# Convolution taps with their chunks, gates and first adds moved, earlier chunk splits, last tile by row tiles

## The chip, the cores and the metric

One core of one Trainium2 chip runs the whole program. The metric is the time of one execution on the device in microseconds (us). TensorE does matmuls and transposes, VectorE (DVE in the rows), ScalarE (ACT), GpSimd (POOL) and SyncE (SP) work beside it, each in its own order, and semaphores hold one engine until another has got somewhere.

## The reference

A trunk of two layers over 256 rows of width 2048, all in float32. Cut to what matters here:

```python
u = x @ ev_w_in                      # layer 0: 12 column tiles of 512
h = a * sigmoid(gate); h = causal_depthwise_conv(h, width=31)
a_out = silu(layer_norm(h))
b_out = hgrn2(q, f, i, g) * gnorm_g * silu(g)
x = layer_norm(ALPHA * x + concat(a_out, b_out) @ ev_w_out)
x = layer_norm(ALPHA * x + square(relu(x @ w1)) @ w2)
# layer 1: the same, with two kinds of attention heads in place of conv and hgrn2
```

## The kernel before

**Matmuls.** A float32 product is made of three faster ones. Each operand is split into a high part and a rest, and TensorE adds hi x hi, hi x lo and lo x hi (lines 1326 to 1328). Weights stream through in *chunks* of 256 x 512 (512 KB). A chunk s is loaded by SP into one of four raw buffers, ScalarE copies it to `w_hi` (line 493, in the MLP line 716), VectorE subtracts to get `w_lo` (line 802, in the MLP line 1199), and TensorE then does 12 matmuls of 128 x 512 with it, six for each of the two row tiles r (rows 0 to 127 and 128 to 255). SP may load chunk s once `w_lo` of chunk s - 4 is made. Both `w_hi` and `w_lo` of a chunk wait until TensorE is done with the chunk that lay in the same place: chunk s - 4 at first, chunk s - 8 where the ring is eight deep. In layer 0 that begins at chunk 120. `upto(s)` is the call on ScalarE and VectorE that splits every chunk up to s; all their other work is placed by hand between such calls.

**Stages of a layer.** Chunks 0 to 95 are the 12 input tiles. Chunks 96 to 127 are the output projection in three parts: part 0 (chunks 96 to 103, two a tile), part 1 (104 to 119, four a tile) and part 2 (120 to 127). Part 2 uses the last four heads' output, which TensorE transposes behind chunk 117 ("O1", line 1398), ScalarE copies to `c_hi` (line 508, called as `group_hi`) and VectorE completes as `c_lo` (line 814, `group_lo`). Then the MLP: 4 blocks of 8 tiles of 8 chunks, from chunk 128 on. Accumulators are two, used in turn, so that tile t + 2 waits until VectorE has added tile t to X (`add_row`, lines 827 and 830, for both row tiles).

**Beside it in layer 0.** The convolution is 248 *taps* on VectorE (line 1067, 128 x 256 each). `taps_behind(s)` gives how many follow chunk s, four or five, two while the recurrence runs. `forget(half, s0)` turns the forget gates to a cumulative sum: a maximum (line 976), a logarithm on ScalarE (line 575), and a scan on VectorE (line 980). It is called inside the loop at s = 31 and s = 79 and splits two chunks more on its way. The recurrence has seven levels and two more: VectorE makes decays (line 993), weighs (lines 1007 and 1008), TensorE multiplies (line 1481) and VectorE takes the scores (line 1022). `gates(half)` (line 1034) multiplies the output gate by its norm weights, needed at chunk 117.

**MLP.** The first product of a tile is taken out by ScalarE with relu (line 710) and squared (line 712), and TensorE transposes it (line 1712) in the middle of the next tile. A tile's 8 chunks are worked in two halves of four: row tile 0 of the half, then row tile 1 of it.

**End.** `last_norm` (line 926) adds the last tile, takes the statistics, and for each piece of a row tile subtracts the mean (`centre`, line 864) and scales (`scale`, line 870). SP then stores that piece (line 363). `STORES` has two pieces of 1024 columns for row tile 0 and four of 512 for row tile 1. The reciprocal root comes from GpSimd (line 413).

## Time and profile before

| what | us |
|---|---|
| median of 3 runs | 2288.47 |
| their range | 2286.49 to 2291.45 |
| profiled execution | 2288.11 |
| its span, first to last instruction | 2286.4 |
| TensorE busy with matmuls in the span | 2249.9 |
| VectorE busy | 1341.9 |
| ScalarE busy | 1057.0 |
| load of a weight chunk, issue to landing, medians of its groups | 3.7 to 4.7 |

The span leaves out 1.7 us of the execution's time. Matmuls overlap in the rows (each is shown with 0.39 us, and starts about 0.23 us after the one before), so the gap between two starts tells more than the busy time.

### The profile page before, as it was taken

To read this page: it belongs to the slowest core of one execution; us is meant where nothing else is said; L and a number is where in the kernel's file an instruction comes from. 1 tells how busy PE (TensorE), PEld (TensorE's weight loads), DVE (VectorE), ACT (ScalarE), POOL (GpSimd) and SP (SyncE) were. 2 spreads that over 40 slices of the span, in tenths; PEclk is the share of its full clock that TensorE was granted. 3 is DMA by queue.
4 is the path that set the end of the run, shared out by engine and by line. 5 is a ranking of instruction groups with operands and counts; after the bars stand their busy time and mean duration, and the time that the engine had idled before them with its cause. 6 is when DMAs were issued, how large, how long until landed. Compare 5 with 4: busy or idle time off the path is not lost.

```text
span 2286.4 us, 28509 instructions
## 1 busy us (share of the span) xinstructions
PE 2249.9 (98%) x10331; PEld 1864.2 (82%) x10331; DVE 1341.9 (59%) x1472; ACT 1057.0 (46%) x1146; POOL 36.6 (2%) x68
## 2 busy tenths in 40 slices
PE   8999999999999999999999999999999999999997
PEld 7888788788888888888878888887888888888886
DVE  4898986854445544445565445568454454544455
ACT  4555565454344444344434444444534444543541
POOL 2000000000000001000000000000000000000000
PEclk9999999999999999999999999999999999999999
DMA  7555545565556656655546555565555565555553
GB/s 242 166 158 158 172 133 177 164 209 190 196 184 221 194 190 199 207 185 184 186 127 193 166 177 165 164 227 156 190 190 195 184 221 195 183 193 200 184 184 110
DMA packets 213040, 418.50 MB, mean 183 GB/s; under 512 B 12793, under 2 KB 13361, under 8 KB 211904
## 3 DMA queue, kind: packets, MB, share of 16 engines
q1 hardware_dynamic: 211120, 406.90, 55.8%
q0 software_dynamic: 1808, 10.04, 1.3%
q8 instruction: 78, 1.28, 0.2%
q14 instruction: 34, 0.28, 0.0%
HBM read 414.79 MB, written 2.10 MB: 182 GB/s over the span
## 4 chain that ended last, share of the span: by engine, by line
PE 91%; DVE 4%; DMA 2%; ACT 1%; issue 1%; DVEq 0%; SPq 0%; ACTq 0%
PE gemm L1326 29%; PE gemm L1328 29%; PE gemm L1327 29%; PE pair L1712 1%; DVE w_lo L802 1%; DVE lnp L1067 1%; DMA raw<-in_mlp_w 1%; PE pair L1481 1%; ACT w_hi L493 1%; PE pair L1398 1%; PE pair L1438 0%; PE pair L1554 0%; PE pair L1626 0%; PE pair L1599 0%; DVE X L864 0%
## 5 line engine op out<-in xcount | busy, mean ns | idle before, releaser
L1199 DVE TENSOR_TENSOR w_lo<-raw,w_hi 128x1024 fp32r<-128x1024 f32 x488 | 596.7, 1225 | 484.7 <-ACT w_hi L716 453.6
L716 ACT ACTIVATE w_hi<-raw 128x1024 fp32r<-128x1024 f32 x492 | 522.1, 1061 | 631.4 <-PE gemm L1328 608.7
L1326 PE MATMUL gemm<-w_hi,x_hi 128*128 128x512 f32 x1792 | 710.4, 396 | 7.0 <-DVE w_lo L802 6.5
L1328 PE MATMUL gemm<-w_hi,x_lo 128*128 128x512 f32 x1792 | 701.1, 391 | 0.0
L1327 PE MATMUL gemm<-w_lo,x_hi 128*128 128x512 f32 x1792 | 700.3, 391 | 0.0
L1326 PE MATMUL gemm<-w_hi,c_hi 128*128 128x512 f32 x1280 | 502.0, 392 | 4.6 <-DVE X L830 3.4
L1328 PE MATMUL gemm<-w_hi,c_lo 128*128 128x512 f32 x1280 | 499.6, 390 | 0.0
L1327 PE MATMUL gemm<-w_lo,c_hi 128*128 128x512 f32 x1280 | 499.5, 390 | 0.0
L802 DVE TENSOR_TENSOR w_lo<-raw,w_hi 128x1024 fp32r<-128x1024 f32 x280 | 340.3, 1223 | 199.3 <-ACT w_hi L493 193.5
L493 ACT ACTIVATE w_hi<-raw 128x1024 fp32r<-128x1024 f32 x276 | 289.3, 1056 | 305.8 <-PE gemm L1328 268.9
L1326 PEld LDWEIGHTS gemm<-w_hi,x_hi 128*128 128x128 f32 x1792 | 338.0, 189 | 82.3 <-issue 6.1
L1328 PEld LDWEIGHTS gemm<-w_hi,x_lo 128*128 128x128 f32 x1792 | 337.8, 189 | 71.2
L1327 PEld LDWEIGHTS gemm<-w_lo,x_hi 128*128 128x128 f32 x1792 | 338.3, 189 | 66.9
L1326 PEld LDWEIGHTS gemm<-w_hi,c_hi 128*128 128x128 f32 x1280 | 241.4, 189 | 54.8 <-DVE X L830 3.9
L1328 PEld LDWEIGHTS gemm<-w_hi,c_lo 128*128 128x128 f32 x1280 | 241.1, 188 | 50.3
L1327 PEld LDWEIGHTS gemm<-w_lo,c_hi 128*128 128x128 f32 x1280 | 241.5, 189 | 49.3
L1171 DVE SCALAR_TENSOR_TENSOR X<-X,factor,gemm 128x512 f32<-128x512 f32 x64 | 47.6, 744 | 100.5 <-PE gemm L1328 100.5
L1067 DVE SCALAR_TENSOR_TENSOR lnp<-scr,lnp 128x256 f32<-128x256 f32 x240 | 100.6, 483 | 0.0
L1184 DVE TENSOR_TENSOR c_lo<-pair,c_hi 128x1024 fp32r<-128x1024 f32 x32 | 39.2, 1225 | 91.4 <-ACT c_hi L703 91.3
L703 ACT ACTIVATE c_hi<-pair 128x1024 fp32r<-128x1024 f32 x32 | 32.9, 1027 | 98.1 <-PE pair L1712 98.1
L710 ACT ACTIVATE scr<-gemm 128x1024 f32<-128x1024 f32 x32 | 32.9, 1028 | 8.1 <-PE gemm L1328 8.1
L1712 PEld LDWEIGHTS pair<-ident,scr 128*128 128x128 f32 x256 | 29.9, 141 | 7.6 <-ACT scr L712 3.6
(194 smaller groups left out, 784.3 us busy)
## 6 DMA issues: line engine op xcount, KB each, us to landing
raw<-in_mlp_w SPq DMA_DIRECT2D x512, 512.0 KB, 4.7
raw<-in_ev_w_in SPq DMA_DIRECT2D x96, 512.0 KB, 3.8
raw<-in_od_w_in SPq DMA_DIRECT2D x96, 512.0 KB, 4.1
raw<-in_ev_w_out SPq DMA_DIRECT2D x32, 512.0 KB, 4.1
raw<-in_od_w_out SPq DMA_DIRECT2D x32, 512.0 KB, 3.7
lnp<-in_ln_mix_g POOLq DMA_DIRECT2D x2, 1024.0 KB, 6.4
lnp<-in_ln_mix_b POOLq DMA_DIRECT2D x2, 1024.0 KB, 6.3
lnp<-in_ln_mlp_g POOLq DMA_DIRECT2D x2, 1024.0 KB, 7.9
```

The lines of the kernel that those rows point to most:

```text
L493: act.activation(hi_of_chunk(s), raw[:, s % RING], ACT.Copy).then_inc(hi_ready, 1)
L703: act.activation(c_hi[:, 4 * (i - 1):4 * i, :], quad[0], ACT.Copy).then_inc(h_hi, 1)
L716: act.activation(hi_of_chunk(s), raw[:, s % RING], ACT.Copy).then_inc(hi_ready, 1)
L802: dve.tensor_tensor(lo_of_chunk(s), raw[:, s % RING], hi_of_chunk(s).bitcast(F32), ALU.subtract).then_inc(lo_ready, 1)
L1067: ins = dve.scalar_tensor_tensor(out=cv[:, ch, :], in0=src, scalar=cw[:, ch, j:j + 1], in1=cv[:, ch, :], op0=ALU.mult, op1=ALU.add)
L1171: dve.scalar_tensor_tensor(out=Xj, in0=Xj, scalar=factor[:, bass.ds(b, 1)], in1=gemm[t % 2][:, r, :], op0=ALU.mult, op1=ALU.add).then_inc( ...
L1184: dve.tensor_tensor(c_lo[:, 4 * (i - 1):4 * i, :], quad[0], c_hi[:, 4 * (i - 1):4 * i, :].bitcast(F32), ALU.subtract).then_inc(h_ready, 1)
L1199: dve.tensor_tensor(lo_of_chunk(s), raw[:, s % RING], hi_of_chunk(s).bitcast(F32), ALU.subtract).then_inc(lo_ready, 1)
L1326: pe.matmul(acc[:, r, :], hi[:, k + c, rows], high, start=begin, stop=False)
L1327: pe.matmul(acc[:, r, :], hi[:, k + c, rows], low, start=False, stop=False)
L1328: return pe.matmul(acc[:, r, :], lo[:, k + c, rows], high, start=False, stop=end)
L1712: ins = pe.transpose(quad[0][:, cc, r * P:(r + 1) * P], urow[(i - 1) % 2][:, r, cc * P:(cc + 1) * P], ident[:, :])
```

## The change

Six edits, in the order of the program:

- `upto_with_taps` stands in for `upto` in VectorE's `forget`. The taps that belong to the chunks split there are done behind each of them, and no longer all after the scan.
- In layer 0, `gates(1)` goes from chunk 101 to chunk 109. In both layers, the adds of part 0's four tiles go ahead of the split of chunk last + 3, where they stood ahead of last + 4 (last is a tile's last chunk).
- At chunk 120 of layer 0 ScalarE and VectorE split chunks 121, 122 and 123 before they take "O1" out, and not after.
- In the first MLP tile of each layer, ScalarE's relu and square stand ahead of one chunk copy more (the third of four, not the fourth).
- TensorE works the very last tile of the program by row tiles: all eight chunks for row tile 0, then all eight for row tile 1.
- In `last_norm` the four pieces of row tile 1 are centred two ahead of the scaling and not four, and the stores of pieces 3 and 5 are issued by ScalarE.

```diff
+ON_ACT = (3, 5)
...
             for i, (r, k0, n_) in enumerate(STORES):
-                sp.wait_ge(normed, 3 * NO + i + 1)
+                if i not in ON_ACT:
+                    sp.wait_ge(normed, 3 * NO + i + 1)
...
                 if s == OUT_SLOT[1]:
+                    upto(s + RING - 1)
                     group_hi("O1", 12)
...
-            def mlp_tile(base, tbase, layer, b, i, splits=range(CPT)):
+            def mlp_tile(base, tbase, layer, b, i, splits=range(CPT), relu_at=CPT - 1):
...
-                    if i < NT and c == CPT - 1:
+                    if i < NT and c == relu_at:
...
-                    mlp_tile(base, tbase, layer, 0, i, splits=range(CPT) if i else range(RING, CPT))
+                    mlp_tile(base, tbase, layer, 0, i, splits=range(CPT) if i else range(RING, CPT),
+                             relu_at=CPT - 1 if i else CPT - 2)
...
+            for i in ON_ACT:
+                r, k0, n_ = STORES[i]
+                act.wait_ge(normed, 3 * NO + i + 1)
+                cols = slice(k0 * P, (k0 + n_) * P)
+                act.dma_start(out[0, r * P:(r + 1) * P, cols], X[:, r, cols]).then_inc(stored, 16)
...
-                            if s == (last + RING if last + RING < DEEP0[layer] else last + DEEP):
+
+                            behind = DEEP if last + RING >= DEEP0[layer] else RING if part else RING - 1
+                            if s == last + behind:
...
-                c = [centre(*piece) for piece in STORES[2:]]
+                c = [centre(*piece) for piece in STORES[2:4]]
                 rstd_wait(4, 1)
-                for piece, centred in zip(STORES[2:], c):
-                    scale(*piece, centred)
+                for piece, behind in zip(STORES[2:], STORES[4:] + [None, None]):
+                    scale(*piece, c.pop(0))
+                    if behind:
+                        c.append(centre(*behind))
...
             def forget(half, s0):
-                upto(s0 + 15)
+                upto_with_taps(s0 + 15)
...
-                upto(s0 + 17)
+                upto_with_taps(s0 + 17)
...
-            taps = [0]
+            taps, tap_slot = [0], [22]
+
+            def taps_upto(s):
+
+                while tap_slot[0] <= min(s, MEAN_SLOT + 2):
+                    conv(taps_behind(tap_slot[0]))
+                    tap_slot[0] += 1
+
+            def upto_with_taps(s):
+                while at[0] <= s:
+                    upto(at[0])
+                    taps_upto(at[0] - 1)
...
-                if s == 101:
+                if s == 109:
                     gates(1)
...
                 if s == OUT_SLOT[1]:
+                    upto(s + RING - 1)
                     group_lo(12, 3)
-                if 22 <= s < MEAN_SLOT + 3:
-
-                    conv(taps_behind(s))
+                taps_upto(s)
...
-                    for half in range(CPT // RING):
+
+                    length = CPT if layer == DEPTH - 1 and last_block and i == 2 * NT - 1 else RING
+                    for half in range(CPT // length):
                         for r in range(RT):
-                            for c in range(RING * half, RING * (half + 1)):
+                            for c in range(length * half, length * (half + 1)):
```

What stands where on VectorE at the second `forget` (chunks 79 to 83; `w_lo` is a chunk's split, `lnp<-scr,lnp` a tap, `scr<-rstm,scr` the scan), before:

```order
L802 TENSOR_TENSOR w_lo<-raw,w_hi 128x1024
L976 TENSOR_SCALAR scr<-scr 128x1024
L802 TENSOR_TENSOR w_lo<-raw,w_hi 128x1024 x2
L980 SCALAR_TENSOR_TENSOR scr<-rstm,scr 128x1024
L1067 SCALAR_TENSOR_TENSOR lnp<-scr,lnp 128x256 x13
L802 TENSOR_TENSOR w_lo<-raw,w_hi 128x1024
```

And of the change (its lines are numbered otherwise):

```order
L811 TENSOR_TENSOR w_lo<-raw,w_hi 128x1024
L989 TENSOR_SCALAR scr<-scr 128x1024
L811 TENSOR_TENSOR w_lo<-raw,w_hi 128x1024
L1091 SCALAR_TENSOR_TENSOR lnp<-scr,lnp 128x256 x9
L811 TENSOR_TENSOR w_lo<-raw,w_hi 128x1024
L1091 SCALAR_TENSOR_TENSOR lnp<-scr,lnp 128x256 x4
L993 SCALAR_TENSOR_TENSOR scr<-rstm,scr 128x1024
L811 TENSOR_TENSOR w_lo<-raw,w_hi 128x1024
```

The 13 taps have gone ahead of the scan, nine of them ahead of the split of chunk 81; between the splits of chunks 80 and 82 stand the same instructions as before. The first `forget` changes in the same way.

VectorE from chunk 118 to chunk 128 of layer 0 (`X<-gemm,X` is an add, `c_lo<-pair,c_hi` is `group_lo`), before:

```order
L802 TENSOR_TENSOR w_lo<-raw,w_hi 128x1024
L830 TENSOR_TENSOR X<-gemm,X 128x512 x2
L802 TENSOR_TENSOR w_lo<-raw,w_hi 128x1024 x2
L814 TENSOR_TENSOR c_lo<-pair,c_hi 128x1024
L802 TENSOR_TENSOR w_lo<-raw,w_hi 128x1024 x6
L830 TENSOR_TENSOR X<-gemm,X 128x512 x2
L802 TENSOR_TENSOR w_lo<-raw,w_hi 128x1024 x2
```

And of the change:

```order
L811 TENSOR_TENSOR w_lo<-raw,w_hi 128x1024
L839 TENSOR_TENSOR X<-gemm,X 128x512 x2
L811 TENSOR_TENSOR w_lo<-raw,w_hi 128x1024 x5
L823 TENSOR_TENSOR c_lo<-pair,c_hi 128x1024
L811 TENSOR_TENSOR w_lo<-raw,w_hi 128x1024 x3
L839 TENSOR_TENSOR X<-gemm,X 128x512 x2
L811 TENSOR_TENSOR w_lo<-raw,w_hi 128x1024 x2
```

Three splits have moved from behind `group_lo` to ahead of it; the adds of part 1's last tile still stand behind the split of chunk 126. ScalarE's copies move in the same way about `group_hi`.

## Rows read from the trace of the kernel before

**Rows 1.** Waits of TensorE over the span: total us, times, longest
```profile
PE gemm L1326 <- DVE w_lo L802: 6.5, 8, 3.4
...
PE pair L1712 <- ACT scr L712: 2.8, 2, 1.6
PE pair L1481 <- DVE scr L1022: 2.2, 2, 1.6
...
PE gemm L1326 <- DVE X L827: 1.1, 1, 1.1
```

**Rows 2.** Windows: busy time of each engine; PEclk is the granted clock
```profile
268.10:273.60 5.50, 5.46 (x13) 4.19 (x14) 5.50 (x11) 0.00 (x0) 0.00 (x0) 0.50 0.56 178
...
346.00:349.00 3.00, 3.00 (x9) 2.42 (x9) 0.74 (x2) 2.99 (x5) 0.00 (x0) 0.51 0.37 104
...
414.90:420.40 5.50, 5.48 (x13) 4.32 (x14) 5.43 (x7) 1.16 (x2) 0.00 (x0) 0.50 0.84 257
...
470.00:476.00 6.00, 6.00 (x31) 5.10 (x32) 4.64 (x4) 4.73 (x5) 0.00 (x0) 1.00 0.71 217
1273.80:1277.30 3.50, 3.50 (x10) 2.69 (x9) 0.00 (x0) 0.00 (x0) 0.00 (x0) 0.52 0.43 143
```

**Rows 3.** Timeline of VectorE at the two scans: start, duration, [idle before, releaser]
```profile
100.88 1.23 DVE L802 TENSOR_TENSOR w_lo<-raw,w_hi 128x1024 fp32r<-128x1024 f32 x1 [1.79 <-ACT w_hi L493]
...
258.40 1.22 DVE L802 TENSOR_TENSOR w_lo<-raw,w_hi 128x1024 fp32r<-128x1024 f32 x1 [0.94 <-ACT w_hi L493]
...
261.74 5.21 DVE L1067 SCALAR_TENSOR_TENSOR lnp<-scr,lnp 128x256 f32<-128x256 f32 x13
266.87 1.22 DVE L802 TENSOR_TENSOR w_lo<-raw,w_hi 128x1024 fp32r<-128x1024 f32 x1
```

**Rows 4.** Timeline of VectorE, chunks 101 to 105
```profile
338.34 1.22 DVE L1034 TENSOR_TENSOR scr<-scr,lnp 128x1024 f32<-128x1024 f32 x1
...
343.20 0.70 DVE L1022 COPY_PREDICATED scr<-masks,pair 128x512 f32<-128x512 int8 x1
...
354.61 1.27 DVE L827 SCALAR_TENSOR_TENSOR X<-X,gemm 128x512 f32<-128x512 f32 x2
```

**Rows 5.** Timelines by engine, chunks 120 to 127; last row from the critical chain
```profile
414.92 0.79 PE L1326 MATMUL gemm<-w_hi,c_hi 128*128 128x512 f32 x1 [3.44 <-DVE X L830]
...
411.35 1.06 ACT L493 ACTIVATE w_hi<-raw 128x1024 fp32r<-128x1024 f32 x1 [2.01 <-DMA raw<-in_ev_w_out]
...
401.69 1.22 DVE L814 TENSOR_TENSOR c_lo<-pair,c_hi 128x1024 fp32r<-128x1024 f32 x1 [2.90 <-ACT c_hi L508]
...
413.58 1.28 DVE L830 TENSOR_TENSOR X<-gemm,X 128x512 f32<-128x512 f32 x2
...
397.55 1.63 SPq L323 DMA_DIRECT2D raw<-in_ev_w_out  x2
...
405.20 6.12 DMA raw<-in_ev_w_out
```

**Rows 6.** Timeline of ScalarE in the first MLP tile of layer 0
```profile
466.87 1.06 ACT L716 ACTIVATE w_hi<-raw 128x1024 fp32r<-128x1024 f32 x1 [0.81 <-DMA raw<-in_mlp_w]
...
468.87 1.06 ACT L712 ACTIVATE scr<-scr 128x1024 f32<-128x1024 f32 x1
```

**Rows 7.** Timelines of TensorE, VectorE and SP's queue at the program's end
```profile
2274.49 0.39 PE L1328 MATMUL gemm<-w_hi,c_lo 128*128 128x512 f32 x1
...
2255.48 1.21 DVE L1199 TENSOR_TENSOR w_lo<-raw,w_hi 128x1024 fp32r<-128x1024 f32 x1
...
2269.47 0.75 DVE L1171 SCALAR_TENSOR_TENSOR X<-X,factor,gemm 128x512 f32<-128x512 f32 x1 [12.79 <-PE gemm L1328]
...
2276.20 0.74 DVE L1171 SCALAR_TENSOR_TENSOR X<-X,factor,gemm 128x512 f32<-128x512 f32 x1
...
2280.73 2.73 DVE L870 SCALAR_TENSOR_TENSOR X<-X,rstd,lnp 128x512 f32<-128x512 f32 x4
...
2282.83 0.99 SPq L363 DMA_DIRECT2D out<-X  x2
```

More of the change, by code:

```diff
@@ L360, in _ @@
             for i, (r, k0, n_) in enumerate(STORES):
-                sp.wait_ge(normed, 3 * NO + i + 1)
-                cols = slice(k0 * P, (k0 + n_) * P)
-                sp.dma_start(out[0, r * P:(r + 1) * P, cols], X[:, r, cols]).then_inc(stored, 16)
+                if i not in ON_ACT:
+                    sp.wait_ge(normed, 3 * NO + i + 1)
+                    cols = slice(k0 * P, (k0 + n_) * P)
+                    sp.dma_start(out[0, r * P:(r + 1) * P, cols], X[:, r, cols]).then_inc(stored, 16)
             sp.wait_ge(stored, 16 * len(STORES))
@@ L779, in _ @@
             mlp(1)
+            for i in ON_ACT:
+                r, k0, n_ = STORES[i]
+                act.wait_ge(normed, 3 * NO + i + 1)
+                cols = slice(k0 * P, (k0 + n_) * P)
+                act.dma_start(out[0, r * P:(r + 1) * P, cols], X[:, r, cols]).then_inc(stored, 16)
         @block.vector
```

## Prediction

> **What bounds the kernel.** Matmuls do: TensorE is busy for 2249.9 of 2286.4 us, and the change leaves every one of them in. So an edit is worth what it takes from the places where TensorE stands still or runs slowly, and I read those first. The list of TensorE's waits is short [rows 1]: of the 6.5 us for `w_lo` one wait is 3.4, the waits for ScalarE's square are 1.6 and 1.2, those for the scores 1.6 and 0.6, and an add of line 827 costs 1.1. The longest of all is the 3.44 us before the matmul at 414.92 [rows 5]. Next come the windows behind these waits, for the clock [rows 2]. Behind both long waits the granted clock is 0.50 for 5.5 us, its level of 1.2 GHz in place of 2.4, and half of such a stretch is lost: 2.75 us. Waits of 1.6 us go both ways: behind the one for the scores the clock is 0.51 for 3.0 us (1.5 lost), behind the one before the transposes at 469.98 it is 1.00. At 1273.8 it is 0.52 for 3.5 us with no wait of TensorE's shown ahead. So a wait has a second price of 0 to 2.75 us, and this is the largest unknown here. Last I read the timelines of VectorE, ScalarE and SP's queue about each wait, since the edits move work there.
>
> **Taps with their chunks.** At the second scan VectorE is busy without a break except for 0.94 us ahead of the split at 258.40 [rows 3]. Chunk 82's split, at 266.87, is what TensorE waits 3.4 us for. The change puts nine taps into that break, 5.21/13 = 0.40 us each, 3.6 us in all. Between the splits of chunks 80 and 82 stand the same instructions as before, so only the break is saved: chunk 82 is ready 0.94 us earlier, and a wait of about 2.5 us stays. Chunk 81's split moves from 258.40 to about 260.9 and ends near 262.1. TensorE wants that chunk two chunks before 264.6 plus one, at 261.9, so 0.2 us of the wait falls there. It is the same total. What the clock makes of 2.5 us lies between the 3.4 us wait (2.75 lost) and the 1.6 us one (0 or 1.5): I take 2.15, that is 0.6 back. Term: 0.94 + 0.6 = **1.5**; bounds 0.9 (nothing back) and 3.7 (all back).
>
> At the first scan the break is 1.79 us [rows 3], and VectorE works without idle from there to the scores, where TensorE waits 0.6 [rows 1]. The nine taps fill it, VectorE comes to the scores 1.8 us earlier, and that wait goes. Term: **0.6**; bounds 0 and 0.8. None of it carries on to the second scan, as VectorE waits for ScalarE and TensorE in between.
>
> **Gates and first adds.** `gates(1)` at 338.34 [rows 4] stands ahead of the scores at 343.20, for which TensorE waits 1.6. Moving it away would take 1.2 off. But the order shows that the adds of part 0's second tile, 1.27 us, come to stand in the same place (ahead of the split of chunk 102). 1.22 out, 1.27 in: that wait and the slow stretch behind it stay. Term: **0**; bounds -0.2 and 1.2. The adds of the third tile stand at 354.61 behind the convolution's `c_lo` [rows 4], and TensorE's 1.1 us wait is for them. One split earlier they run at about 346.6, behind chunk 103's split and in ScalarE's shadow, so the wait goes. Two chunks on, the fourth tile's adds now stand ahead of the recurrence's last weighing, and TensorE, 1.1 us earlier, meets the scores of level six 0.2 us too soon. Term: **0.9**; bounds 0.3 and 1.1. In layer 1 TensorE waits nowhere in part 0. There the adds now hold the split behind them until a tile is done, which still leaves a split (1.2 us) and two adds (1.3) within the two chunks of matmuls (5.4) that TensorE has ready. Cost 0; it would be what the split is late if that cover went. The moved `gates(1)` at chunk 109 falls into VectorE's idle there: 0.
>
> **Chunks split ahead of the last group.** Before, TensorE waits at chunk 122 until the add at 413.58 (two of 0.64 us) is done [rows 5]; that add is queued behind the split of chunk 126, this behind its copy at 411.35, and this behind a load that took from 405.20 to 411.3, since SP may issue it only when chunk 122 is split. And chunk 122 was split late because VectorE sat idle for 2.90 us in front of `group_lo` (401.69). With three splits ahead, chunks 121 and 122 use that idle. I work it out with 4.5 us from issue to landing, an estimate: the page of the profile has medians of 3.7 to 4.7 us for the weights' loads, and chunk 126's 6.1 is the long end, met by GpSimd's parameter rows on the same engines. Then 121 and 122 are split near 400.3 and 402.4, 3.7 and 2.8 us earlier; 125's load lands at 404.8 and 126's at 407 to 408.5; the split of 126 ends near 409.7 and the adds near 411. TensorE wants them at 411.3. The wait of 3.44 falls to 0 to 0.6, and with it goes the slow stretch of 2.75 behind it. The new price: `group_hi` is queued behind the copy of chunk 123, whose load is issued at 397.55 [rows 5] and lands near 402. The copy ends at 403.1, `group_hi` at 404.1, the split of 123 at 404.3, `group_lo` at 405.5. TensorE wants the group for chunk 120, 24 matmuls before 411.3, at 405.9. It fits by 0.4. Behind that, VectorE's adds for chunks 129 to 131 come some 3.3 us earlier while TensorE comes 6 earlier, out of 2.5 us of slack, so about 0.2 may come back as a wait. Term: 3.44 + 2.75 less 0.5 for these remainders = **5.7**; bounds 2.5 (waits of 1.5 at both places, half of the clock back) and 6.2.
>
> **Relu ahead of one copy more.** Before, ScalarE copies a chunk at 466.87 which it had waited for (DMA), then does relu and, from 468.87 for 1.06, the square [rows 6]; TensorE starts the transposes at 469.98 after 1.6 us idle. Relu needs only tile 0, finished by 463. One copy earlier (1.0 us), and without the 0.81 us of waiting ahead of it, the square ends near 468.1, and TensorE wants it at 468.4. The same holds in layer 1 for its 1.2 us. The chunk that is copied later is wanted more than 5 us on. Term: 1.6 + 1.2 = **2.8**; bounds 2.0 and 2.8, as the clock was not slow behind them.
>
> **The last tile.** Row tile 1's last matmul starts at 2274.49, and row tile 0's add starts at 2269.47, 24 matmuls before the end of row tile 1, whose sums stand 0.4 us behind its last matmul's start, at 2274.9. But VectorE takes them only at 2276.20 [rows 7], being busy with row tile 0 until then. By row tiles, row tile 0 is done at 2264.0 and its 6.7 us of work end near 2270.8, so row tile 1 starts at 2274.9: 1.28 us gained. TensorE needs the last chunks' `w_lo` sooner for this, two chunks of rows before 2264.0 at the latest, and the last of them is made by 2255.48 + 1.21 = 2256.7. From the add to the end of the last `scale`, the same instructions: 2280.73 + 2.73 = 2283.46, so 7.26 us, as two centres (1.3 us) still cover GpSimd's 1.0. The last store then takes 2.9 us to the end of the span at 2286.4. Its row at 2282.83 shows two issues within 0.99 us [rows 7], so SP issues as fast as pieces come. The pieces now come 1.3 us apart and not 0.66, so less stands in front of the last: 0.2. Term: 1.28 + 0.2 = **1.5**; bounds 1.0 (ScalarE issues more slowly than SP, 0.3) and 1.9. The Trainium skill, "DMA: Bandwidth & Descriptors", section "Issuing engines are not separate DMA queues", says that transfers issued from several engines run on the same 16 DMA engines, and that only the time of issuing is saved. By that the two queues bring nothing here; with this the trace agrees, and the term rests on the pieces' spacing.
>
> **Sum.** 1.5 + 0.6 + 0 + 0.9 + 5.7 + 2.8 + 1.5 = 13.0 us from the profiled 2288.11, so 2275.1; that execution lies 0.36 below the median of 2288.47, so I forecast **2275.3**.
>
> **Rivals.**
> *The last group takes the wait over* (0.16). A load lands after 6.1 us as chunk 126's did: chunk 123's copy then ends at 404.8 and `group_lo` at 407.2, 1.3 us late, and chunk 126 is late by as much. For it: two loads share the DMA engines with GpSimd's parameter rows there. Against it: chunk 123's load is issued before those rows are. The term falls to about 2, and the time is 2279.
> *The stall at chunk 122 does not move* (0.06): another load binds it. Then 13.0 - 5.7 = 7.3: 2281.
> *The clock gives more back* (0.10): the shortened wait no longer costs a slow stretch (2.15 more), and the one at 346 falls away too as its moment shifts (1.5): 2271.5. The Trainium skill's page "TensorE: Matmul & The Clock Gate", section "Why this matters for your kernels", holds that throughput drops come from idle gaps that are long enough and that shortening them avoids it; by that page the 2.5 us wait costs no clock. The 1.6 us wait with a slow stretch behind it speaks against it, so it has no more than this chance.
> *Slower* (0.02): the adds that now stand ahead of splits hold `w_lo` back until TensorE runs dry. The nearest case is chunk 105 of layer 0, split by 355.8 and wanted at 357.6. It decides from 1.8 us of lateness on; each such place would cost what the second scan's did, 3.4 + 2.75 = 6.2. With eight tiles, three of them at once outweigh 13: 2294.
>
> **Chances.** The forecast has 0.66, with a range of its own of 2272 to 2278.5. To hold 8 in 10 the range takes in half of both neighbours: 2270.5 to 2281.5. Some 0.2% (4.6 us) is what a measurement tells from no change, so faster needs less than 2283.9. All cases but the last lie there; single bad terms together with the scatter of 5 us between runs leave 0.05 for no difference.
>
> **What would show it.** Right: no wait at chunk 122 and clock 1.00 behind it; a wait of 2 to 2.7 us at the second scan and still one of 1.6 for the scores near 342; no wait before the first transposes of line 1712; the last tile's add 0.43 us behind the last matmul's start. Wrong: a wait for `c_lo` at chunk 120 of over 0.5 us, waits at chunks 100 to 107, slow clock in new places, or a last store that takes over 3 us.

## The result and the profile after

The changed kernel takes 2275.2 us, the median of 5 runs (2273.79 to 2277.56), where the kernel before took 2288.47. The ratio is 0.9945, with a 95% interval of 0.9931 to 0.9959. So the kernel is faster: by 13.3 us between the medians, and by 0.55% going by the ratio. The forecast of 2275.3 holds.

The sum in the prediction went by one profiled execution, so it is held against one here. The changed kernel's profiled execution took 2273.79 us. Ahead of each fence stands what view it is. First, the head of the profile's page: the span, and busy time with share and instructions of each engine.

```profile
span 2272.1 us, 28509 instructions
...
PE 2242.8 (99%) x10331; PEld 1858.2 (82%) x10331; DVE 1341.5 (59%) x1472; ACT 1056.6 (47%) x1146; POOL 36.3 (2%) x68
```

The span fell by 14.3 us, from 2286.4. VectorE and ScalarE do the same work as before within 0.4 us. Only the places where TensorE stands still or runs slowly have changed. The list of TensorE's waits of the changed kernel, to be held against [rows 1] (total us, times, longest):

```profile
PE gemm L1349 <- DVE w_lo L811: 5.5, 10, 1.8
PE pair L1461 <- DVE X L881: 1.9, 4, 0.8
PE pair L1504 <- DVE scr L1035: 1.7, 2, 1.5
PE gemm L1349 <- DVE X L839: 1.0, 1, 1.0
PE gemm L1349 <- DVE x_lo L823: 1.0, 1, 1.0
PE gemm L1349 <- issue: 0.5, 1, 0.5
PE pair L1504 <- DVE scr L1021: 0.5, 1, 0.5
```

The line numbers moved: 1349 to 1351 are the matmuls, 811 is `w_lo`, 1035 the scores, 1021 a weighing of the recurrence, 1091 the taps, 839 the adds of part 2, 715 the square. The waits for the square are gone, and the 3.4 us for the add at chunk 122 has become 1.0. But `w_lo` has ten waits now and not eight, the one for a weighing is 0.5 where it was 0.2, and two are new: 0.5 at chunk 120 (issue), and 1.0 for `x_lo` at 17.61, at the start of the program, which six of the twelve variants below don't have. To see where the gain arises, I took the starts of the weight matmuls in both traces, counted in order, twelve to a chunk: "chunk 80" is the start of the first of its twelve. In the MLPs, where a half of four chunks is worked row tile by row tile, 138 and 522 are so the start of row tile 1 in the halves that begin with chunks 136 and 520, and 767 is the start of the last twelve matmuls. "Gain" is the start before less the start after, worked out from these rows of matmuls:

```
chunk                         36    44    80    83    90    94    96   102   108
gain, us                    0.43  2.26  2.30  5.88  5.94  3.73  3.72  4.00  4.45
chunk                        118   120   124   128   136   138   384   418   420
gain, us                    4.45  3.77  8.72  7.89  7.76  9.46  9.40  9.39 10.98
chunk                        510   512   520   522   640   767   end of the span
gain, us                   10.98 11.92 11.98 13.37 13.18 12.96  14.3
```

A rise is a place where the change gives something, and a fall is a place where it is taken back. The falls behind chunks 90, 118 and 124 are what the sum did not have.

**Second scan.** TensorE's and VectorE's timelines about chunk 82 (start, duration, [idle before, releaser]), against [rows 3]:

```profile
264.85 0.50 PE L1349 MATMUL gemm<-w_hi,x_hi 128*128 128x512 f32 x1 [1.84 <-DVE w_lo L811]
...
255.11 3.65 DVE L1091 SCALAR_TENSOR_TENSOR lnp<-scr,lnp 128x256 f32<-128x256 f32 x9
...
261.38 2.29 DVE L993 TENSOR_TENSOR_SCAN scr<-rstm,scr 128x1024 f32<-128x1024 bf16 x1
263.59 1.21 DVE L811 TENSOR_TENSOR w_lo<-raw,w_hi 128x1024 fp32r<-128x1024 f32 x1
```

The nine taps now lie ahead of the scan, and chunk 82's split starts at 263.59 where it started at 266.87: 3.28 us earlier, 2.30 of them because TensorE itself runs 2.3 us ahead here. The 3.4 us wait is 1.84, with 0.20 more at chunk 81. Then two windows, the second-scan stage behind the wait and the recurrence behind that (columns: window, us, then busy time and instructions of PE, PEld, DVE, ACT, POOL, then PEclk, the granted clock):

```profile
264.80:270.00 5.20, 5.15 (x26) 4.32 (x27) 5.20 (x10) 3.52 (x4) 0.00 (x0) 1.00 0.54 162
...
268.00:291.00 23.00, 22.56 (x104) 18.47 (x102) 23.00 (x42) 11.04 (x12) 0.00 (x0) 1.00 0.60 183
```

In the first the clock is 1.00, the 2.4 GHz level, where the kernel before had 0.50 behind its wait [rows 2]. In the second VectorE is busy for 23.00 of 23.00 us: it sets the pace. TensorE has got 3.6 us ahead through the shorter wait and the clock, and it meets VectorE at chunks 91 and 92:

```profile
291.26 0.50 PE L1349 MATMUL gemm<-w_hi,x_hi 128*128 128x512 f32 x1 [0.70 <-DVE w_lo L811]
294.81 1.97 PE L1504 MATMUL pair<-scr 128*128 128x64 f32 x16 [0.51 <-DVE scr L1021]
```

**Last group.** The waits of TensorE about chunks 120 to 122, VectorE's adds, and the piece of the critical chain that is chunk 126's load, against [rows 5]:

```profile
402.11 0.47 PE L1349 MATMUL gemm<-w_hi,c_hi 128*128 128x512 f32 x1 [0.52 <-issue]
408.87 0.50 PE L1349 MATMUL gemm<-w_hi,c_hi 128*128 128x512 f32 x1 [1.05 <-DVE X L839]
...
400.79 1.22 DVE L823 TENSOR_TENSOR c_lo<-pair,c_hi 128x1024 fp32r<-128x1024 f32 x1
...
407.53 1.28 DVE L839 TENSOR_TENSOR X<-gemm,X 128x512 f32<-128x512 f32 x2
...
397.85 7.42 DMA raw<-in_ev_w_out
...
409.00:415.00 6.00, 6.00 (x27) 4.96 (x28) 5.93 (x8) 2.44 (x4) 0.00 (x0) 1.00 0.81 256
```

`c_lo` ends at 402.0, and TensorE starts chunk 120 with it at 402.11 after 0.52 us. The adds wait behind chunk 126's split, and its load took 7.42 us, where I had reckoned with 4.5. The clock behind the wait is 1.00.

**Relu.** There is no wait for line 715 left. ScalarE does relu at 458.36 and the square at 459.40, with no copy waited for in between; against [rows 6]:

```profile
457.39 1.06 ACT L719 ACTIVATE w_hi<-raw 128x1024 fp32r<-128x1024 f32 x1 [1.56 <-DMA raw<-in_mlp_w]
458.36 1.02 ACT L713 ACTIVATE scr<-gemm 128x1024 f32<-128x1024 f32 x1
459.40 1.06 ACT L715 ACTIVATE scr<-scr 128x1024 f32<-128x1024 f32 x1
```

**End.** The last matmul, the last tile's add for row tile 1, the last scales and ScalarE's last store, against [rows 7]:

```profile
2261.52 0.39 PE L1351 MATMUL gemm<-w_hi,c_lo 128*128 128x512 f32 x1
...
2261.95 0.75 DVE L1194 SCALAR_TENSOR_TENSOR X<-X,factor,gemm 128x512 f32<-128x512 f32 x1 [4.06 <-PE gemm L1351]
...
2267.80 1.41 DVE L881 SCALAR_TENSOR_TENSOR X<-X,rstd,lnp 128x512 f32<-128x512 f32 x2
...
2269.24 0.34 ACTq L788 DMA_DIRECT2D out<-X  x1
```

The add follows the last matmul's start by 0.43 us, as it was to be. From it to the end of the last scale it is 7.26 us (2269.21 less 2261.95), and from there to the end of the span 2.9: both as before.

**What this execution had and others have not.** Two rises belong to no edit: 1.59 between chunks 418 and 420, where the kernel before had a stretch at 0.52 [rows 2] and this one has not, and 0.94 between 510 and 512. There the kernel before waits 0.85 us ahead of the transposes in layer 1's norm, and so do all twelve variants below (0.59 to 1.14 us); this one profile doesn't. Together they are 2.5 of the 14.3 us. The other 11.8 lie where the edits act, the 0.4 of the start apart. How much of that another execution may have differently is seen below, from kernels whose instructions are the same up to chunk 136.

### The profile page after: what moved, and what is told of

Same layout as the page of the kernel before. It is cut to its first block, busy times and chain, and to the rows that moved or that the text cites. A ratio compares the mean times of both kernels' runs of the same rounds, so it can differ in the third digit from the quotient of the medians.

```text
span 2272.1 us, 28509 instructions
## 1 busy us (share of the span) xinstructions
PE 2242.8 (99%) x10331; PEld 1858.2 (82%) x10331; DVE 1341.5 (59%) x1472; ACT 1056.6 (47%) x1146; POOL 36.3 (2%) x68
## 3 DMA queue, kind: packets, MB, share of 16 engines
q8 instruction: 78, 1.28, 0.2%
## 4 chain that ended last, share of the span: by engine, by line
PE 91%; DVE 5%; issue 1%; ACT 1%; DMA 1%; SPq 0%; POOL 0%; DVEq 0%; ACTq 0%
PE gemm L1349 29%; PE gemm L1351 28%; PE gemm L1350 28%; DVE lnp L1091 1%; PE pair L1735 1%; DVE w_lo L811 1%; PE pair L1504 1%; ACT w_hi L495 1%; DMA raw<-in_ev_w_out 1%; PE pair L1421 1%; PE pair L1461 0%; DMA raw<-in_ev_w_in 0%; PE pair L1577 0%; PE pair L1649 0%; PE pair L1622 0%
## 5 line engine op out<-in xcount | busy, mean ns | idle before, releaser
L520 ACT ACTIVATE x_hi<-pair 128x512 fp32r<-128x512 f32 (+1 forms) x30 | 15.3, 511 | 43.6 <-PE pair L1461 43.6
```

## The experiments

Theory A: each edit gives what its stage shows, but a stage in which VectorE or a load sets the pace takes part of it back, since TensorE arrives there sooner. The rival, B: the gains add up as the prediction's terms did, and the two falls belong to one edit alone or vary from run to run. All variants are made from the changed kernel. Where I compare positions, "later" and "earlier" is the start of a chunk against the changed kernel's, less the difference at chunk 36 (up to 0.4 us either way, the start of the program). Each kernel has one profile.

### Taps after the scans again

```diff
-                upto_with_taps(s0 + 15)
+                upto(s0 + 15)
...
-                upto_with_taps(s0 + 17)
+                upto(s0 + 17)
```

> The changed kernel with the taps after each scan again. Theory A (VectorE sets TensorE's pace from chunk 36 to 94, so that only VectorE's own 1.8 us and 0.94 us count, and the clock got back behind the second scan is lost again in waits at chunks 91 to 94): a wait of 3.4 us at chunk 82 with a slow stretch behind it, no waits at chunks 91 to 94, and TensorE 2.8 us later at chunk 96; 2278.0. Theory B (what the clock gives back stays): 5.9 us later at chunk 96, 2281.

Measured: 2278.91 us (2278.31 to 2281.12), 0.9961 [0.9947, 0.9975] of the kernel before. TensorE's wait at chunk 82 and the clock behind it:

```profile
267.52 0.79 PE L1349 MATMUL gemm<-w_hi,x_hi 128*128 128x512 f32 x1 [3.40 <-DVE w_lo L811]
...
268.00:273.00 5.00, 5.00 (x13) 3.73 (x13) 5.00 (x10) 0.00 (x0) 0.00 (x0) 0.50 0.67 195
```

The 3.4 us wait and the slow stretch are back, and chunk 83 starts 5.4 us later: 1.8 from the first scan, 3.6 from the second. By chunk 96 it is 3.2, as the waits at chunks 91 to 94 are gone. So the taps' edit gives 5.4 and the stage behind takes 2.2 back. That is A (2.8 forecast for chunk 96, against 5.9 by B). It also sizes the first scan: 1.8 us, not 0.6. TensorE's list of waits names 0.6 and 0.2 there. The distances from chunk to chunk, worked out from the matmuls' starts, tell the rest. Three of them in three kernels:

```
from chunk to the next   36->37  37->38  39->40
before                     2.98    2.89    2.98
taps after the scans       2.95    2.85    3.03
changed kernel             2.72    2.72    2.72
```

Each matmul is shown with 0.39 us and the next starts 0.23 later. So a delay is listed some 0.16 short: a distance of 0.55 between two starts, 0.32 more than usual, is listed as a wait of 0.16. Distances of 0.43 and 0.50 are not listed as waits at all.

### Eight taps left out

The four taps behind chunk 85 and those behind 86 aren't done, so this kernel leaves out eight of the convolution's 248 taps. It asks whether VectorE's work sets the pace up to chunk 94.

```diff
-                    conv(taps_behind(tap_slot[0]))
+                    if tap_slot[0] in (85, 86):
+                        taps[0] += taps_behind(tap_slot[0])
+                    else:
+                        conv(taps_behind(tap_slot[0]))
```

> The changed kernel without the eight taps behind chunks 85 and 86 (the convolution leaves them out), 3.2 us less work for VectorE just behind the second scan. Theory A: the waits at chunks 91 to 94 (0.70, 0.51, 0.20 us) go and TensorE is 2.1 us earlier at chunk 96; 2273.1. Rival: those waits come from the chain through ScalarE's exponentials, which taps do not touch: the same waits, 2275.2.

Measured: 2274.17 us (2272.6 to 2275.01), 0.9936 [0.992, 0.9953]. The waits at 91 to 94 are gone and chunk 96 starts 2.2 us earlier. So VectorE was the pace, and this fall is explained. But against the changed kernel's profile the gain is lost again from there: 1.1 us by chunk 108, with a second wait for scores of 1.18 at 346.67, and the wait at chunk 122 is 2.14 in place of 1.05:

```profile
408.32 0.50 PE L1352 MATMUL gemm<-w_hi,c_hi 128*128 128x512 f32 x1 [2.14 <-DVE X L839]
```

Chunk 124 starts only 0.5 us earlier. That may be a second cap, or a difference between two executions; the last comparison of positions, under the early taps with the late row, takes this up.

### No chunks split ahead of the last group

```diff
                 if s == OUT_SLOT[1]:
-                    upto(s + RING - 1)
```

(on ScalarE and on VectorE)

> The changed kernel with chunks 121 to 123 split after the last group again. Theory A (VectorE and the norm behind part 2 cap what TensorE gains here): a wait of about 3.4 us at chunk 122 with 5.5 us of half clock behind it, TensorE 4 to 5 us later at chunk 124 but only 3.4 us later at chunk 136; 2278.6. Theory B (the term of the prediction, all of it kept): 5.7 us later at both, 2280.9.

Measured: 2279.02 us (2276.41 to 2279.56), 0.9957 [0.994, 0.9974]. The wait at chunk 122 is back, longer than before the change, with a slow stretch behind it:

```profile
411.31 0.79 PE L1347 MATMUL gemm<-w_hi,c_hi 128*128 128x512 f32 x1 [3.98 <-DVE X L838]
...
411.30:417.00 5.70, 5.69 (x13) 4.45 (x14) 5.63 (x7) 1.25 (x3) 0.00 (x0) 0.50 0.86 256
```

By chunk 136 it is 4.1 us later. At chunk 124 it was 5.0. So undone alone the edit is worth 4.1, and 3.3 between the two kernels, not the 5.7 of the forecast.

### Gates and first adds back

```diff
-                            behind = DEEP if last + RING >= DEEP0[layer] else RING if part else RING - 1
+                            behind = DEEP if last + RING >= DEEP0[layer] else RING
...
-                if s == 109:
+                if s == 101:
                     gates(1)
```

> The changed kernel with gates(1) at chunk 101 and the first adds one chunk later again. Theory A (gates and the second tile's adds trade places, so only the third tile's adds count): the wait for the scores behind chunk 101 stays at 1.5 us, a wait of 1.1 us for the add at chunk 104 is back, TensorE 0.6 us later at chunk 108; 2275.8. Rival (the early adds cost VectorE somewhere): no change or earlier at chunk 108, 2275.2 or less.

Measured: 2277.47 us (2276.45 to 2279.35), 0.9955 [0.9938, 0.9972]. The wait for scores at 340.13 is unchanged (1.60, the changed kernel 1.54), so there the two moves do trade places. Behind it stand two waits that the changed kernel's profile doesn't have:

```profile
340.13 2.00 PE L1504 MATMUL pair<-scr 128*128 128x64 f32 x16 [1.60 <-DVE scr L1035]
...
348.75 2.00 PE L1504 MATMUL pair<-scr 128*128 128x64 f32 x16 [1.09 <-DVE scr L1035]
352.06 0.50 PE L1349 MATMUL gemm<-w_hi,c_hi 128*128 128x512 f32 x1 [1.31 <-DVE X L836]
```

Chunk 108 starts 2.3 us later. 1.3 of it is the wait for the third tile's adds (line 836), the one in the sum. The other, 1.09 for the next scores, is not this edit's: it stands, as 1.16 to 1.18, in five profiles more in which the slow stretch of this stage falls behind it, among them two of kernels with the same instructions up to here as the changed one (row tiles and stores undone, both 1.17). In the changed kernel's profile that stretch lies at 342 to 346, ahead of these scores, and TensorE comes late enough for them. So undone alone the edit costs about 1.3 (2.3, where those two start chunk 108 1.0 later), and the profiles of the two kernels differ by 0.7 in this stage.

### GpSimd's row loaded later

To tell whether chunk 126's load is long because of GpSimd's parameter row (2048 values for each of 128 partitions, 1 MB), which is issued at 396.45, the row waits here until chunk 126 is split.

```diff
+            pool.wait_ge(lo_ready, 127)
             row(lnp[:, 1, :], ln_mix_b[0], D, lnp_loaded)
```

> The changed kernel with GpSimd's second parameter row (1 MB) held back until chunk 126 is split. Theory A (that row shares the DMA engines and makes chunk 126's load take 7.4 us): the load takes 4.5 to 5 us, the wait of 1.05 us at chunk 122 goes, TensorE 1 us earlier at chunk 124, some of it lost in the norm; 2274.4. Rival (the weights' own loads in flight slow each other): 7 us and 1 us of wait as before, 2275.2.

Measured: 2275.37 us (2272.75 to 2276.14), 0.9945 [0.993, 0.996]. The row's issue, ScalarE's copy of chunk 126 (at 405.29 in the changed kernel) and the adds:

```profile
405.57 0.53 POOL L380 DMA_DIRECT2D lnp<-in_ln_mix_b  x1 [21.37 <-DVE w_lo L812]
...
402.69 1.06 ACT L496 ACTIVATE w_hi<-raw 128x1024 fp32r<-128x1024 f32 x1 [0.21 <-DMA raw<-in_ev_w_out]
...
404.93 1.28 DVE L840 TENSOR_TENSOR X<-gemm,X 128x512 f32<-128x512 f32 x2
```

The load, issued at 397.59, took 5.1 us and not 7.4, and the adds (line 840 here) start at 404.93 and not at 407.53. The 7.4 is the short end: in the eight other variants that keep these splits and the row where it was, the row is issued 1.1 to 1.7 us ahead and the load takes 7.7 to 8.5. The waits at chunks 120 and 122 are both gone, and chunk 124 starts 2.0 us earlier, chunk 136 2.2. So this contention was what the last group's term lacked: with the row held back chunks 118 to 136 give 5.4 (3.3 and 2.1), near the 5.7 of the forecast. The medians don't show the gain (2275.37 and 2275.20, with ranges of 3.4 and 3.8 us). The wait of 1.13 us in layer 1's norm, which the changed kernel's profile lacks, takes half of it back between the two profiles; whether it does between the medians, no profile tells. So what is shown is the load's time and the positions in the trace, not a faster kernel.

### Second tile's adds one chunk later

```diff
-  ... else RING if part else RING - 1
+  ... else RING if part or (layer == 0 and j == 1) else RING - 1
```

> The changed kernel with the adds of part 0's second tile in layer 0 one chunk later again, so that nothing takes the place of gates(1). Theory A (gates and these adds traded places): the wait for the scores behind chunk 101 falls from 1.54 to 0.3 us and TensorE is 1.2 us earlier at chunk 102; the slow stretch behind it goes (1.7 us more) or moves; 2272.5 to 2274. Rival: the wait moves on to the next level's scores, and nothing is left at chunk 108; 2275.2.

Measured: 2276.87 us (2275.67 to 2277.51), 0.995 [0.9935, 0.9966]. The waits for the two levels' scores:

```profile
338.87 2.00 PE L1504 MATMUL pair<-scr 128*128 128x64 f32 x16 [0.33 <-DVE scr L1035]
...
348.79 2.63 PE L1504 MATMUL pair<-scr 128*128 128x64 f32 x16 [2.40 <-DVE scr L1035]
```

The first falls from 1.54 to 0.33, and the next takes it over at 2.40; chunk 102 starts 1.2 us earlier, chunk 108 0.8 later. The adds were what the scores waited for. Moving them moves the wait.

### Eight taps moved ahead

Two taps more behind each of chunks 61 to 64, where VectorE has idle time, so that the stage behind the second scan has eight fewer.

```diff
-    return 2 if LEVEL_SLOT[0] <= s <= LEVEL_SLOT[0] + 20 else 4 + (s % 4 == 0)
+    return 2 if LEVEL_SLOT[0] <= s <= LEVEL_SLOT[0] + 20 else 4 + (s % 4 == 0) + 2 * (61 <= s < 65)
```

> The changed kernel with eight taps moved from chunks 89 to 91 to chunks 61 to 64, where VectorE had 3.5 us idle; nothing is left out. Theory A (VectorE's work up to chunk 94 is the cap, and a second cap stands at chunk 122): no waits at chunks 91 to 94, TensorE 2.1 us earlier at chunk 96, but only 0.5 us earlier at chunk 124; 2274.6. Rival: the eight taps make splits late at chunks 65 to 82, the wait at the second scan grows, and nothing is gained.

Measured: 2275.77 us (2274.42 to 2276.4), 0.9945 [0.993, 0.996]. As with the taps left out: no waits at 91 to 94, chunk 96 2.1 us earlier, then 1.18 at the second scores and 1.52 at chunk 122, and chunk 124 only 0.1 earlier. Chunk 126's load, from the critical chains of the changed kernel and of this one (issue, us to landing):

```profile
397.85 7.42 DMA raw<-in_ev_w_out
...
396.25 8.54 DMA raw<-in_ev_w_out
```

It is issued 1.6 us sooner and lands 0.5 sooner: the load's own time took the rest.

### The last three together, and two of them

```diff
+    return 2 if LEVEL_SLOT[0] <= s <= LEVEL_SLOT[0] + 20 else 4 + (s % 4 == 0) + 2 * (61 <= s < 65)
...
+            pool.wait_ge(lo_ready, 127)
...
+  ... else RING if part or (layer == 0 and j == 1) else RING - 1
```

The last line is in the kernel with all three only.

> The three edits of late_row, second_back and early_taps together. Theory A (three caps in a row, each of which hid the next): their gains add, 2.1 + 1.2 + 1.0 and what the clock gives, less 1 us in the norm; 2271.5. Rival (the norm behind part 2 or the MLP's first loads cap it all): 2274.5, no better than the best of the three.

Measured: 2274.42 us (2272.49 to 2277.57), 0.9941 [0.9928, 0.9955]. The second scores wait 2.40 us again, with half clock behind them:

```profile
346.56 3.67 PE L1505 MATMUL pair<-scr 128*128 128x64 f32 x16 [2.40 <-DVE scr L1036]
...
350.00:353.00 3.00, 3.00 (x9) 2.42 (x9) 3.00 (x5) 0.00 (x0) 0.00 (x0) 0.50 0.53 175
```

The gains do not add: the time is the rival's 2274.5 and not the 2271.5 of three caps. Against the changed kernel chunk 102 starts 3.2 us earlier, chunk 108 0.2 later, chunk 124 1.2 earlier, and chunk 128 as in the changed kernel, with waits of 0.54 for an add at 416.40 and 1.12 in the norm on the way. What makes the adds late at 416.40 was not followed up.

Without the third, that is with early taps and the late row:

> The edits of early_taps and late_row together, second_back left out. By the caps seen so far: TensorE 1.0 us earlier at chunk 108 (early_taps alone had that) and, with chunk 126's load no longer slowed, 2 us more at chunk 124, so 3 us earlier there; 2272.5. Rival (the norm behind part 2 is the next cap): 2 us earlier at chunk 136 as late_row alone, 2273.5 or more.

Measured: 2273.56 us (2271.5 to 2275.32), 0.994 [0.9926, 0.9953], span 2269.8. TensorE's longest waits in layer 0's projections are the two for scores:

```profile
PE gemm L1350 <- DVE w_lo L812: 5.2, 9, 1.8
PE pair L1462 <- DVE X L882: 2.9, 5, 1.0
PE pair L1505 <- DVE scr L1036: 2.7, 2, 1.6
```

Chunk 124 starts 3.2 us earlier than in the changed kernel, chunk 136 3.3. The late row alone gave 2.0 at chunk 124 and the early taps alone 0.1. That looks like two caps in a row, the second hiding what the first edit frees. But one profile of each can't show it. The changed kernel and the ones with relu, row tiles and stores undone (below) have the same instructions up to chunk 136, and they differ as much. Worked out from the matmuls' starts, us later than in the changed kernel:

```
chunk                              83    96   108   118   124   136
relu where it was                 0.0   0.0   0.0   0.0   0.7   0.6
last tile in halves               1.5   0.0   1.0   1.0   1.7   1.7
all stores on SP                  1.5   0.0   1.0   1.0   1.1   1.1
early taps                        0.0  -2.1  -1.0  -1.0  -0.1  -0.2
late row                          0.0   0.0   0.0   0.0  -2.0  -2.2
early taps and late row           0.0  -2.0  -1.1  -1.1  -3.2  -3.3
```

The changed kernel's profile is the earliest of the four at chunk 124. In two of them TensorE waits 1.17 us for the second scores, as in the three profiles with the taps moved ahead or left out and the second tile's adds in place (1.16 to 1.18):

```profile
348.54 1.22 PE L1504 MATMUL pair<-scr 128*128 128x64 f32 x9 [1.17 <-DVE scr L1035]
```

And their waits at chunk 122 are 1.05, 1.58, 1.97 and 1.35 us, with 7.4, 8.1, 8.1 and 7.7 us for chunk 126's load. Against the mean of the four (0.9 us later than the changed kernel's at chunk 124) the early taps give 1.0, the late row 2.9 and both 4.1: so taken, the gains nearly add (1.0 and 2.9 for 4.1). The falls that B puts down to the execution are there at chunks 108 and 124. So two things are shown, VectorE's pace up to chunk 94 and the load's contention with the row; a second cap that hides the first edit's gain is not. The kernel with both has the lowest median of all kernels here that do all the work, 1.6 us below the changed kernel's 2275.2, but the ranges overlap, so faster than the changed kernel is not shown.

### Relu where it was

```diff
-                             relu_at=CPT - 1 if i else CPT - 2)
+                             relu_at=CPT - 1)
```

> The changed kernel with relu ahead of the fourth copy again in the first MLP tiles. The term of the prediction, 2.8 us: waits of 1.6 and 1.2 us before the first transposes of the two MLPs are back, TensorE 1.6 us later behind chunk 137 and 1.2 us more behind the same tile of layer 1; 2278.0. Rival (part of it is caught up by loads that come sooner): 1 us or less; 2276.

Measured: 2279.06 us (2277.45 to 2285.15), 0.9967 [0.9955, 0.9979], span 2276.0. The waits are back in both layers:

```profile
PE pair L1735 <- ACT scr L715: 2.6, 2, 1.5
```

From chunk 136 to 138 TensorE loses 1.2 us against the changed kernel, from 520 to 522 1.7: 2.9 in all, as forecast (2.8). The rest of the span's 3.9 is mostly the wait in layer 1's norm, 1.14 here.

### The last tile in halves again

```diff
-                    length = CPT if layer == DEPTH - 1 and last_block and i == 2 * NT - 1 else RING
+                    length = RING
```

> The changed kernel with the last tile in halves again, its two store queues kept. The term of the prediction: VectorE takes the last tile's second row tile 1.28 us later, at 1.7 us behind the last matmul's start; 2276.5. Rival (row tile 0's stores are in the way of row tile 1's when both come late): 2277 or more.

Measured: 2278.08 us (2275.68 to 2278.87), 0.9955 [0.994, 0.9971], span 2275.7. The last matmul starts at 2263.90, and row tile 1's add only when row tile 0's scales are done:

```profile
2263.23 2.48 DVE L881 SCALAR_TENSOR_TENSOR X<-X,rstd,lnp 128x1024 f32<-128x1024 f32 x2
2265.62 0.74 DVE L1194 SCALAR_TENSOR_TENSOR X<-X,factor,gemm 128x512 f32<-128x512 f32 x1
```

The add is 1.72 us behind the matmul and not 0.43. From the start of chunk 767 to the end of the span it is 14.3 us (changed kernel 13.0): 1.3. The other 2.4 us of the span's 3.6 arise far ahead of the edit, in instructions that are the changed kernel's own. Part of that is a slow stretch behind the second scan's wait:

```profile
265.00:268.50 3.50, 3.50 (x10) 2.68 (x10) 3.50 (x8) 2.18 (x2) 0.00 (x0) 0.51 0.65 162
```

It makes chunk 83 1.5 us later, but chunk 96 not at all: the waits of 0.70 and 0.51 at chunks 91 and 92 are gone in exchange, since VectorE sets the pace there. What stays is 1.0 at the second scores, 0.7 at chunk 122 (chunk 126's load took 8.13 us here) and 1.1 in layer 1's norm, less the shorter start.

### All stores on SP

```diff
-ON_ACT = (3, 5)
+ON_ACT = ()
```

> The changed kernel with all six stores on SP's queue. If only the pieces' spacing counts, the end of the span lies within 0.1 us of the changed kernel's, measured from the last matmul: 2275.2. Rival (the second queue itself brings something): 0.3 us or more later.

Measured: 2276.49 us (2275.84 to 2276.66), 0.9949 [0.9934, 0.9964], span 2274.6. From the start of chunk 767 to the end of the span it is 13.0 us, as in the changed kernel. So the second queue gives nothing. The Trainium skill, "DMA: Bandwidth & Descriptors", section "Issuing engines are not separate DMA queues", says that issuing from several engines saves only the time of issuing, and this agrees. The span is 2.5 us longer for other reasons: 1.1 by chunk 136, in the same places as with the row tiles undone, and 1.6 from a slow stretch at 1265. The clock in the two stretches that the changed kernel's profile lacks:

```profile
265.20:268.20 3.00, 3.00 (x9) 2.34 (x8) 3.00 (x7) 1.92 (x2) 0.00 (x0) 0.50 0.52 175
1265.00:1268.50 3.50, 3.50 (x10) 2.73 (x9) 0.00 (x0) 0.00 (x0) 0.00 (x0) 0.54 0.42 143
```

## Why the prediction was right, and where its terms were off

The total was right, 13.3 us in the medians and 14.3 in the two profiled spans for a sum of 13.0. That it was so close is in part luck: the errors of the terms made up for each other. What a term gave is the difference in gain between the chunks named.

| term | forecast | measured | read from |
|---|---|---|---|
| taps, first scan | 0.6 | 1.8 | chunks 36 to 44 |
| taps, second scan | 1.5 | 3.6 less 2.2 | 80 to 83, 90 to 96 |
| gates and first adds | 0.9 | 0.7 | 96 to 118 |
| last group | 5.7 | 3.3 | 118 to 136 |
| relu | 2.8 | 3.1 | 136 to 138, 520 to 522 |
| last tile | 1.5 | 1.4 | 767 to the end |
| in no term | 0 | 2.5 | 418 to 420, 510 to 512 |

The rest is 0.4 of a shorter start and 0.4 that small steps in the MLPs took. These are differences of two profiles. The three kernels with the same instructions start chunk 118 0.0 to 1.0 us later than the changed one and chunk 136 0.6 to 1.7 later, so the two terms from 96 to 136, 4.0 together, would be 2.3 to 3.5 by them.

- **First scan: mis-sized, 1.8 for 0.6, outside its bounds (0 to 0.8).** The step that failed is "that wait goes": I took the waits that the list shows, 0.6 for the scores, as all that there was to gain. At chunks 36, 37 and 39 TensorE lost 0.2 to 0.3 us each, which the list of idle time doesn't show at all.
- **Second scan: net right, by two errors.** The wait shrank as said, from 3.4 to 1.84 and 0.20. The step "I take 2.15, that is 0.6 back" was wrong: the clock stayed at 1.00 in this profile and in ten of the twelve kernels that have the taps moved (this one and eleven variants), and gave 2.6 back. That was the first half of the third rival; its other half, the slow stretch at 346 gone, did not come. The Trainium skill, "TensorE: Matmul & The Clock Gate", section "Why this matters for your kernels", says that shortening the idle gaps avoids the drop; ten of the twelve agree, and two, with a wait of 1.89 and 0.50 to 0.51 behind it, don't, so by these profiles it avoids it mostly and not always. What undid this was missing in the prediction altogether: VectorE is without idle time from chunk 82 to 91, so it can be ahead by only what it had won itself, and TensorE gives 2.2 us back. The taps left out and the taps moved ahead both remove it. The prediction had asked only where the wait goes, not who sets the pace of the stage behind.
- **Gates and first adds: about right between these two profiles, and by the reasons given.** The wait for the scores stayed at 1.5, and the wait for the third tile's adds, 1.1, went (1.3 when undone). That the next scores may then wait was foreseen with 0.2 and is 1.1 to 1.2 in profiles whose slow stretch falls later. In the two of them with the changed kernel's instructions chunk 108 starts 1.0 later, so that the scatter is as large as the term. The kernel with only the second tile's adds put back shows that these adds are what the scores wait for, and that the next scores take the wait over.
- **Last group: the right mechanism, over-sized.** The step that failed is the estimate of "4.5 us from issue to landing". Chunk 126's load took 7.4, so the adds ended at 408.81 and left a wait of 1.05. Behind that, I had put 0.2 for what the norm might take back, and it took 0.76; all variants with these splits have 0.70 to 0.76 there, the one with all three edits 1.12. I had named GpSimd's parameter rows as what stretched this load before, and then reckoned as if the earlier load would escape them; in fact it was issued at 397.85, 1.4 us behind GpSimd's row. With the row held back it took 5.1, and 2.0 us more were gained at chunk 124. Two of the signs went against me here: "no wait at chunk 122" did not hold, and `c_lo` came late for chunk 120 with a wait of 0.52, just over the 0.5 given for wrong. The clock behind the remaining wait was 1.00, as forecast. The rival "the last group takes the wait over" is what happened by a part.
- **Relu and last tile: right.** 1.2 and 1.7 for the relu undone; 1.3 for the order of row tiles, where 1.28 was forecast. The 0.2 for the stores' spacing did not come: 2.9 us from the last scale to the end in both kernels. With SP alone the end is the same, so the second queue is worth nothing.
- **2.5 us belong to the two profiles compared, not to the edits.** The layer 1 norm's wait is in every other profile, and the slow stretch behind chunk 418 in two of fourteen. The medians are 13.3 apart and not 14.3, as the changed kernel's profiled execution lies 1.4 us under its median and that of the kernel before 0.4 under its own. They can't tell which terms that belongs to.

What stays open: how much of each term between chunks 96 and 136 another pair of executions would give, whether a second cap stands behind VectorE's, why the wait in layer 1's norm varies between 0 and 1.14 us, and what sets the clock back behind a wait of 1.9 us in one profile and not in another with the same instructions.

## What to carry to other kernels

- A gain at one stall reaches the end only through the stages behind it. For each, ask which engine is without idle time there and what its own lead is: here TensorE won 3.6 us at the second scan and gave 2.2 back ten chunks on, where VectorE had no idle time.
- Before a difference between two profiles is put down to an edit, look how far profiles of kernels with the same instructions differ in that stretch. Here it was up to 1.7 us at chunk 124, enough to make two gains that nearly add look like two caps in a row.
- Read a pipelined engine's lateness from start to start of its units of work, not from the list of waits. Here the list showed 0.8 us at the first scan and the starts showed 1.8.
- Before moving a load, look at which other queue's transfers are in flight at the time it moves to, and size it by the long rows if there is one.

## What the runs showed of the hardware

- **A load beside a large row.** Chunk 126's load of 512 KB took 7.4 to 8.5 us in every profile in which GpSimd's 1 MB row was issued 1.1 to 1.7 us ahead of it, and 4.9 to 5.1 in the three kernels where the row came after it. I had expected the range of the page's medians, 3.7 to 4.7, to hold beside the row.
- **The slow stretch between 341 and 357 us moves but doesn't go.** In the kernel before it lies at 346 to 349, in the changed one at 342 to 346, in others up to 357, whatever the waits about it: 0.33 and 2.40, or 1.54 and 1.18, or 1.54 alone. Over the whole window the clock is 0.89 in the versions named below:

```profile
341.00:357.00 16.00, 14.84 (x71) 12.23 (x70) 14.93 (x17) 8.65 (x14) 0.00 (x0) 0.89 0.42 132
```

This is the version with early taps and the late row. The changed kernel, the one before, and those with taps, relu, row tiles or stores undone have 0.89 there as well. The version with all three edits has 0.79: there it is twice as long, from 346 to 353. So a term for "the slow stretch behind this wait goes" was worth nothing here, as the first term of the gates had it.
- **The price of a wait in clock.** Behind 3.4 to 4.0 us (three kernels) it was always 0.50, for some 6 us. Behind 1.84 to 1.89 it was 1.00 ten times and 0.50 to 0.51 for 3 us twice. Behind 1.05 to 2.14 at chunk 122 it was 1.00 in every kernel with such a wait there. And behind chunk 418 it was 0.52 to 0.54 twice with no wait at all.
